# Forgetting attention's softmax steps issued one unit earlier, and its forget-gate chain issued one operation per step

## The reference

```python
h = x + 0.5 * rms_norm(swiglu(rms_norm(x, f1_pre), f1_wg, f1_wu, f1_wd), f1_post)
p_all = rms_norm(h, m_pre) @ w_in
ya, _ = conformer_conv(p_all[..., OFF_A:OFF_B], ...)      # group A: 31 taps per channel, layer norm, silu
yb, _ = gla_mixer(p_all[..., OFF_B:OFF_C], ...)           # group B: gated linear attention in chunks of 64
yc, _ = short_conv(p_all[..., OFF_C:OFF_D], ...)          # group C: 3 taps, gated
q, k, v, logf = fox_project(p_all[..., OFF_D:N_IN], d_bf) # group D: forgetting attention
yd = fox_prompt(q, k, v, logf)                            # or fox_decode for the sampled rows
h = h + rms_norm(concatenate([ya, yb, yc, yd]) @ w_out, m_post)
h = h + 0.5 * rms_norm(swiglu(rms_norm(h, f2_pre), ...), f2_post)

def fox_project(pd, b_f):
    logf = log_sigmoid(pd[..., 3 * hd:] + b_f)
def fox_prompt(q, k, v, logf):            # per block of 128 queries
    c = cumsum(logf)
    s = q @ k.T * scale + c[query] - c[key]               # then masked causally
    o = softmax(s) @ v
```

## Time and profile before

| | |
|---|---|
| median of 3 runs | 1069.25 us (1068.82 to 1069.58) |
| the profiled execution: its own time | 1069.6 us |
| its span in the profile | 1067.8 us, so 1.8 us lie around it |
| PE busy | 1048.1 us, 98% of the span |
| DVE busy | 689.8 us, 65% |
| ACT busy | 571.1 us, 53% |
| POOL busy | 270.8 us, 25% |
| granted TensorE clock | 0.999 of full speed, 9 or more tenths in each of the 40 slices |

### The profile page before, as it was taken

How to read it: one execution, slowest core, us unless ns; L and a number is a source line. 1 busy time by engine, 2 the same in 40 slices (tenths; PEclk the granted TensorE clock), 3 DMA queues, 4 the chain that set the end, 5 groups by cost and what they waited for, 6 DMA issues and landing times. The chain is left out here.

```text
span 1067.8 us, 24171 instructions
## 1 busy us (share of the span) xinstructions
PE 1048.1 (98%) x8956; PEld 1019.6 (95%) x8956; DVE 689.8 (65%) x1029; ACT 571.1 (53%) x969; POOL 270.8 (25%) x338
## 2 busy tenths in 40 slices
PE   6999999999999999999999999999999999999997
PEld 5999999998989999999999999999989999999997
DVE  5666644499986666654476666446999776666443
ACT  5544454477467544454475444546665765444542
POOL 3222220113505222220142222103054232222200
PEclk9999999999999999999999999999999999999999
DMA  7665667443735665656636565764536356565561
GB/s 260 210 182 179 186 207 241 150 142 98 234 92 193 196 180 177 188 169 184 189 122 201 176 192 179 234 198 121 177 103 213 109 175 221 177 189 173 172 188 45
DMA packets 63746, 187.42 MB, mean 176 GB/s; under 512 B 9258, under 2 KB 19506, under 8 KB 63538
## 3 DMA queue, kind: packets, MB, share of 16 engines
q1 hardware_dynamic: 63666, 186.31, 56.3%
HBM read 182.90 MB, written 3.38 MB: 174 GB/s over the span
## 5 line engine op out<-in xcount | busy, mean ns | idle before, releaser
L313 DVE TENSOR_TENSOR w_lo<-raw,w_hi 128x1024 fp32r<-128x1024 f32 (+1 forms) x316 | 411.7, 1308 | 326.8 <-ACT w_hi L303 326.7
L303 ACT ACTIVATE w_hi<-raw 128x1024 fp32r<-128x1024 f32 x336 | 344.4, 1030 | 244.7 <-PE ub L347 170.9
L345 PE MATMUL ub<-hg_hi,w_hi 128*128 128x264 f32 x960 | 276.6, 288 | 0.0
L346 PE MATMUL ub<-hg_lo,w_hi 128*128 128x264 f32 x960 | 272.1, 283 | 0.0
L347 PE MATMUL ub<-hg_hi,w_lo 128*128 128x264 f32 x960 | 271.8, 283 | 0.0
L345 PE MATMUL ub<-act_hi,w_hi 128*128 128x264 f32 x704 | 200.5, 285 | 0.0
L347 PE MATMUL ub<-act_hi,w_lo 128*128 128x264 f32 x704 | 200.0, 284 | 0.0
L346 PE MATMUL ub<-act_lo,w_hi 128*128 128x264 f32 x704 | 199.1, 283 | 0.0
L345 PE MATMUL quad<-hg_hi,w_hi 128*128 128x264 f32 x688 | 196.4, 285 | 0.0
L346 PE MATMUL quad<-hg_lo,w_hi 128*128 128x264 f32 x688 | 194.9, 283 | 0.0
L347 PE MATMUL quad<-hg_hi,w_lo 128*128 128x264 f32 x688 | 194.8, 283 | 0.0
(11 more groups left out here) (250 smaller groups left out, 1308.4 us busy)
## 6 DMA issues: line engine op xcount, KB each, us to landing
raw<-in_w_gu SPq DMA_DIRECT2D x176, 512.0 KB, 4.0
raw<-in_w_dn SPq DMA_DIRECT2D x64, 512.0 KB, 4.0
raw<-in_w_in SPq DMA_DIRECT2D x44, 512.0 KB, 3.7
raw<-in_w_dn SPq DMA_DIRECT2D x32, 384.0 KB, 3.6
raw<-in_w_out SPq DMA_DIRECT2D x16, 512.0 KB, 3.7
pages<-in_cache_k SPq DMA_DIRECT2D x32, 128.0 KB, 3.2
pages<-in_cache_v SPq DMA_DIRECT2D x32, 128.0 KB, 3.1
con<-in_con SPq DMA_DIRECT2D x1, 1192.0 KB
```

The lines of the kernel that those rows point to most:

```text
L303: eng.activation(w_hi[:, slot, 0:w], raw[:, slot, 0:w], ACT.Copy).then_inc(*sig("hi_ready", reps))
L313: eng.tensor_tensor(w_lo[:, slot, 0:w], raw[:, slot, 0:w], w_hi[:, slot, 0:w].bitcast(F32), ALU.subtract)\
L345: eng.matmul(out, a_hi, x_hi[:, k0 + k, :], start=(first and k == 0), stop=False)
L346: eng.matmul(out, a_hi, x_lo[:, k0 + k, :], start=False, stop=False)
```

## The change

It does four things. ACT's softplus of the forget gate goes from step 7 to step 6, ahead of that step's `level_decays`, and DVE's four operations of the chain go from the head of step 9 to the ends of `mix` in steps 7, 8, 9 and 10, one in each. The maxima go from the head of step 20 to step 19 (behind `biased`, ahead of `b_gs` and of the last taps). The exponentials go from step 21 to step 20, ahead of the two copies, which move to step 20 with them. Reciprocals and scaling go from the end of step 21 to the head of its `mix`, ahead of the short convolution and of `rest_unit`. With that, the third head's transposes use `ub[3]` in place of `ub[2]`: the wait for `a_cen` leaves the transposes and comes back ahead of `out`, and `conv_var` waits for the third head's copy as well. No instruction is added or taken away.

```diff
         fox_bank = (mb[0], mb[1], ub[2], mb[2])
+        turned_bank = (mb[0], mb[1], ub[3], mb[0])
@@ PE
             def conv_var(l):
-                after(l, a_sq=1)
+                after(l, a_sq=1, d_pt=3)
@@
                 after(l, d_pn=2 * h + 2)
-                if h == 2:
-                    after(l, a_cen=2)
                 if h == 3:
                     after(l, d_pt=1)
                 for i in range(3):
-                    mm = pe.transpose(fox_bank[h % 3][:, i * P:(i + 1) * P], sm[:, h, i * P:(i + 1) * P], ident)
+                    mm = pe.transpose(turned_bank[h][:, i * P:(i + 1) * P], sm[:, h, i * P:(i + 1) * P], ident)
@@
                 pe.wait_ge(*at(l, "d_pt", 4))
+                pe.wait_ge(*at(l, "a_cen", 2))
                 multiply_first(pe, l, "out", ym_hi, ym_lo, ub, [P] * GROUP, "ym_ready", 0)
@@ ACT
-                if n == 7:
+                if n == 6:
 
                     after(l, proj=2)
                     softplus(l, lft[:, :], proj[0:FGW, FG, :], par[0:FGW, PAR["bf"]:PAR["bf"] + 1], "d_sp")
@@
-                if n == 21:
-                    after(l, d_vT=1)
-                    act.activation(vtok[:, :, :].rearrange("p a b -> p (a b)"), mb[2][:, :], ACT.Copy).then_inc(*sig("d_vt"))
-                    after(l, d_dpT=1)
-                    act.activation(ptd[:, :, :].rearrange("p g r -> p (g r)"), mb[3][:, 0:TP], ACT.Copy).then_inc(*sig("d_ptd"))
+                if n == 20:
                     after(l, d_mx=2)
                     for h in range(H):
 ...
+                    after(l, d_vT=1)
+                    act.activation(vtok[:, :, :].rearrange("p a b -> p (a b)"), mb[2][:, :], ACT.Copy).then_inc(*sig("d_vt"))
+                    after(l, d_dpT=1)
+                    act.activation(ptd[:, :, :].rearrange("p g r -> p (g r)"), mb[3][:, 0:TP], ACT.Copy).then_inc(*sig("d_ptd"))
@@ DVE
-                if n == 9:
-
-                    after(l, d_sp=3, proj=2)
-                    log_sigmoid(l, lf[:, :], proj[0:FGW, FG, :], par[0:FGW, PAR["bf"]:PAR["bf"] + 1], lft[:, :], "d_lf")
-                    after(l, d_lf=2)
-                    dve.tensor_tensor_scan(cf[:, 0:TP], const("ones", TP, FGW), lf[:, 0:TP], 0.0, ALU.mult, ALU.add).then_inc(*sig("d_cf"))
-                    after(l, d_cf=1)
-                    dve.tensor_scalar(cf[:, 0:TP], cf[:, 0:TP], -8.0, None, ALU.mult).then_inc(*sig("d_cf"))
@@ behind level_mask, level_keys and level_exponents of the step
+                if n == 7:
+                    after(l, d_sp=3, proj=2)
+                    dve.tensor_scalar(lf[:, :], proj[0:FGW, FG, :], par[0:FGW, PAR["bf"]:PAR["bf"] + 1], 0.0, ALU.add, ALU.min).then_inc(*sig("d_lf"))
+                if n == 8:
+                    after(l, d_lf=1)
+                    dve.tensor_tensor(lf[:, :], lf[:, :], lft[:, :], ALU.subtract).then_inc(*sig("d_lf"))
+                if n == 9:
+                    after(l, d_lf=2)
+                    dve.tensor_tensor_scan(cf[:, 0:TP], const("ones", TP, FGW), lf[:, 0:TP], 0.0, ALU.mult, ALU.add).then_inc(*sig("d_cf"))
+                if n == 10:
+                    after(l, d_cf=1)
+                    dve.tensor_scalar(cf[:, 0:TP], cf[:, 0:TP], -8.0, None, ALU.mult).then_inc(*sig("d_cf"))
```

More of the change, by code:

```diff
@@ L1007, in probabilities @@
                 after(l, d_pT=h + 1)
-                act.activation(smT[:, h, :], fox_bank[h % 3][:, 0:3 * P], ACT.Copy).then_inc(*sig("d_pt"))
+                act.activation(smT[:, h, :], turned_bank[h][:, 0:3 * P], ACT.Copy).then_inc(*sig("d_pt"))
             def mixer(l):
@@ L1243, in mix @@
                         biased(l, h)
+                    after(l, d_sm=4)
+                    dve.tensor_reduce(stats[:, 0, 0:H], sm[:, :, 0:P], AX.X, ALU.max, negate=True).then_inc(*sig("d_mx"))
+                    dve.tensor_reduce(stats[:, 0, H:2 * H], sm[:, :, P:3 * P], AX.X, ALU.max, negate=True).then_inc(*sig("d_mx"))
                     after(l, b_sg=1)
@@ L1246, in mix @@
                 if n == 20:
-                    after(l, d_sm=4)
-                    dve.tensor_reduce(stats[:, 0, 0:H], sm[:, :, 0:P], AX.X, ALU.max, negate=True).then_inc(*sig("d_mx"))
-                    dve.tensor_reduce(stats[:, 0, H:2 * H], sm[:, :, P:3 * P], AX.X, ALU.max, negate=True).then_inc(*sig("d_mx"))
                     after(l, b_rs=4, b_gs=1)
@@ L1257, in mix @@
                 if n == 21:
+                    for h in range(H):
+                        after(l, d_ex=2 * h + 2)
+                        dve.reciprocal(stats[:, 2, h::H], stats[:, 1, h::H]).then_inc(*sig("d_ri"))
+                        after(l, d_ri=h + 1)
+                        for b, part in ((0, slice(0, P)), (1, slice(P, 3 * P))):
+                            dve.tensor_scalar(sm[:, h, part], sm[:, h, part], stats[:, 2, b * H + h:b * H + h + 1], None, ALU.mult).then_inc(*sig("d_pn"))
                     short_conv(l, 0)
@@ L1287, in behind @@
                     conv_taps(l, *TAPS[n])
[L1288 to L1293, removed]
-                            dve.tensor_scalar(sm[:, h, part], sm[:, h, part], stats[:, 2, b * H + h:b * H + h + 1], None, ALU.mult).then_inc(*sig("d_pn"))
             def short_conv(l, c):
```

## The result

The changed kernel takes 1071.86 us (median of 10 runs, 1070.69 to 1073.83) against 1069.82 for the kernel before (10 runs, 1068.31 to 1070.55): ratio 1.0024, 95% interval 1.0016 to 1.0032. The forecast was 1069.0, its range ended at 1070.4, and "slower" had 0.06. The profiled execution of the changed kernel took 1072.21, its span is 1070.4; one of before had 1067.8.

What follows compares the result with a forecast made beforehand. PE, busy nearly throughout, bounds the kernel, with DVE's gapless queue setting the end of the `in` phase. Per layer -0.27 (forget chain) + 0.14 (maxima) = -0.13, twice -0.26, giving 1069.0 us, range 1067.9 to 1070.4.

Steps and rivals of the forecast that it cites:

- slower: Whole kernel: the outcome of a measurable loss, above 1071.4 us; chance 0.06.
- What bounds the kernel: Only PE's waits can be won, at most 3.1 us; DVE's gapless queue from step 17 sets the `in` phase's end.
- Step 9: Forget chain's old place: PE's 0.64 us wait goes, but DVE's keys wait about 0.8 us for ACT's decays.
- bring DVE to 0.06 late from step 10 on: After step 9's running sum and scaling, DVE's queue is 0.06 us late, not shorter.
- What stays of the gain is 0.27 us: At PE's decoder scores, 0.27 us of the 0.64 won in step 9 remains, per layer.
- From there to unit 16 nothing else is late: From the decoder scores to unit 16 no further delay, so DVE's later queue starts 0.27 us earlier.
- 0 if DVE's lateness in step 6 or 9 is 0.3 us more than I reckon: Lower bound on the forget chain's gain: nothing is left if DVE is that much later.
- The `qd` limit: ACT's last `qd`, which PE's decoder scores need, ends at 788.44, so PE starts at 788.65, not 788.28.
- The maxima: Step 19: they delay unit 19's evacuation, a new 1.01 us PE wait before unit 21, mostly caught: +0.14 per layer.
- The sum: Both layers: -0.27 + 0.14 = -0.13 us per layer, -0.26 in all.
- The rival that ended slower: Unit 21's wait passes through whole and step 9's gain is lost: up to +2.3 us, 1071.5; chance 0.05.
- unit 21 wait: PE waits 1.01 us before unit 21 for DVE's evacuation of unit 19; later waits of 0.87 catch most.

Runs made afterwards that it cites:

- e7: Changed kernel with `a_dec` moved to the head of step 13 and `pm` behind step 16's taps; 1068.81 us, ratio 0.9997 to the kernel before.
- e6: Kernel before with the decode tap products (`smT`), their sum and bias moved behind step 18's taps; 1069.40 us, ratio 0.9999.
- e2: Kernel before with only the softmax part and its banks changed, forget chain left in place; 1069.64 us, ratio 0.9997.
- e1: Kernel before with only the forget chain's new places, softmax left in place; 1072.74 us, ratio 1.0025.
- e9: Changed kernel with GpSimd's subtractions to `w_lo` replaced by zero fills that read nothing; 1067.68 us, ratio 0.9982 to the kernel before.
- e10: Kernel before with GpSimd's subtractions to `w_lo` replaced by zero fills that read nothing; 1069.01 us, ratio 0.9996.
- e5: Changed kernel with each GpSimd subtraction to `w_lo` in four 128x256 instructions, not two of 128x512; 1070.28 us, ratio 1.0010 to the kernel before.
- e12: Kernel before with `a_dec` moved to step 13 and the `pm` products behind step 16's taps; 1069.48 us, ratio 0.9999.
- e8: Changed kernel with `a_pad` and `a_dec` moved to step 10, `pm` behind step 16's taps, decode tap products behind step 18's; 1071.40 us, ratio 1.0020 to before.
- e3: Changed kernel with `a_dec`, `pm` and `dstat` each reading one SBUF tile, leaving out their products; 1071.91 us, ratio 1.0020 to the kernel before.

## Why the prediction was wrong

- *What bounds the kernel* held in part: the stretch changes where PE waits, though PE starts later by somewhat more than the idle time shown (1.26 us for the 1.03 ahead of unit 21 in e7). That DVE's queue from step 17 on sets the end of the phase did not hold: e6 makes it 1.0 us shorter, and all but 0.1 of that goes into a wait for ACT.
- *Step 9* held: PE's 0.64 is gone, DVE's keys wait for ACT's decays there (0.72 for 0.8 forecast) and in step 6 (0.37).
- **The step that failed** is the use of "bring DVE to 0.06 late from step 10 on" for everything behind step 10: "with `qd` at 788.44 + 0.06 + 0.15", "What stays of the gain is 0.27 us" and "From there to unit 16 nothing else is late". The 0.06 itself came out (DVE's `w_lo` of step 10 is 0.07 late). But the lengths of the DVE operations behind it were carried over from the rows of before as if they were DVE's own, and a block by GpSimd was put at nothing without a reason. In its place the runs showed `a_dec` at 1.27 us for 0.18, so that the evacuation of unit 11 is 1.17 us late against level 0 (24.03 for 22.86), of which `a_dec` is 1.09. At L666 PE is 0.81 late in place of 0.27 early, and DVE's idle 0.76 ahead of unit 16's evacuation, forecast at about 0.4, is gone. Another 1.23 are lost at L615, behind `dstat` (1.07 for 0.16). The forecast did name a bound, "0 if DVE's lateness in step 6 or 9 is 0.3 us more than I reckon", but it let lateness eat the gain at most, and it never looked at what POOL does when PE comes 0.6 us earlier.
- *The `qd` limit* is the right place: most of the delay reaches PE there (L666, idle for 0.75), the rest just ahead, where PE loses its 0.71. With the collisions out (e7) PE gets there 787.71 - 753.41 = 34.30 us behind level 0, 0.41 earlier than the 34.71 of before; the forecast was 0.27.
- *The maxima* held: there is a new wait of 0.8 to 1.0 us in e2 and e7, mostly caught by the two waits behind it. Forecast at +0.14 per layer, it costs 0.46 and 0.20 in e2, and 0.10 for both layers together where the changed kernel is set against e1. In the changed kernel the wait is only 0.64. PE is late there and `smT` is blocked for less time, and no run separates the two.
- *The sum* of -0.13 per layer is near what e7 shows with the new collisions out (second layer 79.96 for 80.04, -0.08; first layer -0.30), though e7's ratio, 0.9997, can't be told from 1. So the terms that the forecast had were about right in sum, and one that it lacked, 2.04 per layer, was 15 times as large.
- *The rival that ended slower* had the right sign by the wrong place: it had the unit 21 wait go through whole and the step 9 gain lost. The wait was mostly caught. That its 1071.5 lies near the measured 1071.86 is luck.

Shown are: that the loss belongs to the forget chain (e1, e2), that it is gone when GpSimd's subtractions are fills (e9, e10), that a blocked operation lasts until the end of the other's instruction (e5), and that moving `a_dec` and `pm` undoes the loss (e7, e12). Argued only: that the 0.73 us by which POOL comes earlier is what makes the first collision, since no run held POOL back while PE ran early. Open: the two stretches add 4.07 us, the ratio gives 2.6. In the one profiled execution the rest is the start, since level 0 of the first layer comes at 230.05 before and at 228.60 after, ahead of anything edited. That doesn't explain the medians. e1 has the same gap in its ratio, and its profiled execution was the slowest of its 11. With one profile per kernel nobody can say whether every execution has all the collisions, which hang on clearances of about 0.1 us.

## What to carry to other kernels

The length of a VectorE operation in a trace needn't be its own where GpSimd works beside it (here `a_dec` went from 0.18 to 1.27 us): before an edit that shifts engines against each other, list the two engines' SBUF readers in the stretch and see how near they pass (here `a_dec` had cleared the next subtraction by 0.11 us). Compare busy time at equal instruction counts first; in these traces a block shows there and not as idle time. A wait that is removed from one engine's path moves all that hangs on it, so ask what the earlier engine will now run into.

## What the runs showed of the hardware

- A 128x16 product on VectorE takes 0.18 us alone and 1.27 when it starts while GpSimd subtracts (1.26 to 1.30 us for 128x512); with subtractions of 128x256 (0.74), 0.72. It works both ways: a GpSimd pair takes 2.54 us alone and 3.52 in e7, where its first half starts during a `w_lo` of VectorE and takes 2.10, and its second meets a product too.
- A 128x512 product of two SBUF inputs takes 0.68 to 0.69 us unblocked (e8, e9) and 1.77 in both kernels compared here: what looks like a constant cost was a block, in every layer of both. Elsewhere in both kernels 80 of VectorE's subtractions of 128x1024 start while one of GpSimd's (`act_lo`, 0.76 us) runs; they take 1.7 us (median), the 178 that meet no GpSimd instruction 1.23.
- An operation with one SBUF input in float32 can be blocked as well (1.26 us for 128x16, e3), while one of 128x1 was not (0.15 us inside a subtraction). Reads of PSUM with one of SBUF (0.42 to 0.44) are not.
- Fills on GpSimd (0.53 us for 128x512) neither stretched nor were stretched where they met such operations in e9: four began while VectorE subtracted to `w_lo`, and one `smT` product began inside a fill.
